# Splitting fifteen row buffers between two gather streams: one slot moved from the `v` ring to the `u` ring

## The reference

```python
sc = jnp.einsum('thcd,hcnd->thcn', qry, keys)      # 8 heads, 2 halves, 128 sub-keys
sv, si = lax.top_k(sc, PEER_TOPK)                  # 16 of each half
...
fv, fi = lax.top_k(cand.reshape(...), PEER_TOPK)   # 16 of 256 pairs
gate = jax.nn.softmax(fv, axis=-1)
ue = u[eidx]                                       # 8 x 16 = 128 rows of 1024 for each token
ve = v[eidx]
act = jax.nn.gelu(jnp.einsum('thkd,td->thk', ue, xb))
return jnp.einsum('thk,thkd->td', (gate * act), ve)
```

## Time and profile before

| | |
|---|---|
| median of 3 runs | 3388.74 us (3377.97 to 3389.66) |
| the profiled execution | 3388.74 us, its span 3386.9 us |
| PE (matmuls) busy | 2953.4 us, 87% |
| DVE busy | 2104.8 us, 62% |
| POOL busy | 2073.1 us, 61% |
| ACT busy | 1528.1 us, 45% |
| moved by DMA | 1222.63 MB, mean 361 GB/s |
| mean granted TensorE clock | 0.959 |

### The profile page before, as it was taken

The page is one execution under the profiler, slowest core; times in us unless marked ns, Lnnn a source line. Parts: engine busy times, 40 slices in busy tenths (PEclk is TensorE's granted clock), DMA queues, the critical chain, the costliest instruction groups (busy, mean ns, idle before and its releaser), DMA issues.

```text
span 3386.9 us, 31486 instructions
## 1 busy us (share of the span) xinstructions
PE 2953.4 (87%) x8213; PEld 1396.8 (41%) x8213; DVE 2104.8 (62%) x4852; ACT 1528.1 (45%) x4155; POOL 2073.1 (61%) x2162
## 2 busy tenths in 40 slices
PE   8888999889997899889997898789978997589976
PEld 6754444334443454335443443334433442244221
DVE  2345555856566566856685657766776668364594
ACT  2313653357423663357334753465336633252333
POOL 2003666666656666666667766776677667464675
PEclk9889999999999999999998999999989998798999
DMA  8307999999999999999999999999999999899998
GB/s 313 137 15 270 398 375 361 343 408 405 394 329 388 410 399 372 359 410 405 399 341 389 409 410 396 369 409 409 400 360 410 409 408 356 313 366 340 356 349 349
DMA packets 358876, 1222.63 MB, mean 361 GB/s; under 512 B 42747, under 2 KB 65244, under 8 KB 357404
## 3 DMA queue, kind: packets, MB, share of 16 engines
q0 software_dynamic: 308288, 1121.46, 85.5%
q1 hardware_dynamic: 22540, 66.55, 5.2%
q10 hardware_dynamic: 27872, 32.61, 2.9%
HBM read 1195.69 MB, written 25.79 MB: 361 GB/s over the span
## 4 chain that ended last, share of the span: by engine, by line
PE 47%; DMA 18%; DVE 15%; POOL 7%; issue 7%; ACT 5%; SPq 0%; ACTq 0%; DVEq 0%; POOLq 0%
PE ps L1091 24%; DMA rows<-in_peer_v,idx 11%; PE ps L973 7%; DMA rows<-in_peer_u,idx 5%; PE ps L857 5%; DVE rows L1497 5%; PE ps L956 4%; POOL rows L469 4%; POOL rows L479 3%; PE ps L810 2%; DVE r L1343 1%; DVE r L1338 1%; DVE r L1378 1%; PE ps L833 1%; DVE r L1379 1%
## 5 line engine op out<-in xcount | busy, mean ns | idle before, releaser
L1091 PE MATMUL ps<-rows,diag 128*128 128x512 f32 (+1 forms) x4224 | 2042.5, 620 | 329.8 <-DMA rows<-in_peer_v,idx 152.3
L1497 DVE CUSTOM_DVE_ANT_0 rows<-rows,ps 128x1024 f32<-128x1024 f32 x1056 | 1261.2, 1216 | 638.4 <-DMA rows<-in_peer_u,idx 635.6
L479 POOL DMA_INDIRECT rows<-in_peer_v,idx x1056 | 1028.5, 974 | 602.1 <-PE ps L1091 384.5
L469 POOL DMA_INDIRECT rows<-in_peer_u,idx x1056 | 1019.4, 965 | 603.4 <-issue 258.2
L1091 PEld LDWEIGHTS ps<-rows,diag 128*128 128x128 f32 (+1 forms) x4224 | 779.9, 194 | 1437.2 <-issue 1117.0
L747 ACT ACTIVATE act_g<-act_g 128x1 f32<-128x1 f32 x1056 | 211.0, 200 | 1069.6 <-DVE act_g L1497 1052.2
L753 ACT ACTIVATE diag<-ident,act_g 128x128 f32<-128x128 f32 x1024 | 411.2, 402 | 403.4 <-PE ps L1091 377.4
L749 ACT ACTIVATE act_g<-act_g,gate 128x1 f32<-128x1 f32 x1056 | 311.0, 294 | 34.3
L973 PE MATMUL ps<-w_sc,r 128*128 128x512 f32 (+1 forms) x576 | 282.8, 600 | 1.2 <-ACT r L663 1.2
L857 PE MATMUL ps<-rows 128*128 128x416 f32 (+1 forms) x704 | 242.2, 499 | 0.0
L857 PEld LDWEIGHTS ps<-rows 128*128 128x128 f32 x704 | 133.5, 191 | 106.1 <-issue 65.4
(11 more groups left out here) (269 smaller groups left out, 1836.3 us busy)
## 6 DMA issues: line engine op xcount, KB each, us to landing
rows<-in_w_in ACTq DMA_DIRECT2D x42, 512.0 KB, 6.5
rows<-in_peer_u,idx POOLq DMA_INDIRECT x1056, 8.7
rows<-in_peer_v,idx POOLq DMA_INDIRECT x1056, 8.6
r<-proj SPq DMA_DIRECT2D x7, 1344.0 KB, 10.9
proj<-staged ACTq DMA_DIRECT2D x44, 192.0 KB, 5.7
w_sc<-in_w_q_t SPq DMA_DIRECT2D x8, 1024.0 KB, 8.1
rows<-in_w_in POOLq DMA_DIRECT2D x14, 512.0 KB, 5.7
w_o<-in_w_in POOLq DMA_DIRECT2D x10, 512.0 KB, 7.4
```

The source lines that it names most:

```text
L469: nc.gpsimd.indirect_dma_start(ring[:, slot, :], None, a["peer_u"], bass.IndirectOffsetOnAxis(ap=idx[g % 2][:, k:k + 1], axis=0), engine_s ...
L479: nc.gpsimd.indirect_dma_start(ring[:, slot, :], None, a["peer_v"], bass.IndirectOffsetOnAxis(ap=idx[g % 2][:, k:k + 1], axis=0), engine_s ...
L1091: last = nc.tensor.matmul(Y[j][0:m, :], diag[:, n % DIAGS, 0:m], ring[:, slot, 512 * j:512 * (j + 1)], start=(k == 0), stop=(k == steps_of ...
L1497: V.tensor_tensor_reduce(ring[:, slot, :], ring[:, slot, :], hn_u, 1.0, 0.0, ALU.mult, ALU.add, col).then_inc(S["dots"], 1)
```

## The change

Slot 14 goes from the `v` ring to the `u` ring. The `u` ring then has 5 slots in tile 0, 6 in tiles 1 to 3 and 9 from tile 4; the `v` ring has 4, and 6 from tile 4. The tables `U_SLOTS` and `V_SLOTS` follow from that. Everything else is as before.

```diff
 RING = 15
-U_SETS = {0: (0, 1, 2, 3), 1: (8,), 4: (9, 10, 11)}
-V_SETS = {0: (4, 5, 6, 7, 14), 4: (12, 13)}
+U_SETS = {0: (0, 1, 2, 3, 14), 1: (8,), 4: (9, 10, 11)}
+V_SETS = {0: (4, 5, 6, 7), 4: (12, 13)}
 V_LAG = 2
```

## The result

The changed kernel takes 3413.86 us (median of 4 runs, 3412.94 to 3430.12), the kernel before 3386.98 us (median of 4, 3377.97 to 3389.66): a ratio of 1.0097, 95% interval 1.0075 to 1.0118, (by the two medians alone, 27 us or 0.8% more; the 36 executions of the changed kernel on record have a median of 3417.3 us). The forecast was 3410 us (3372 to 3450). The profiled execution took 3418.86 us, its span 3417.0.

What follows compares the result with a forecast made beforehand. The prediction took DMA gathers (2743 of 3387 us) as the bound, with PE, DVE and POOL's issue close behind. Its terms, -5 + 18 + 3 + 5 = +21 us on 3388.74, gave 3410 us, range 3372 to 3450.

Steps and rivals of the forecast that it cites:

- tile 0: First tile's period: the longer u ring lets POOL run a step further under DVE's pauses, a gain of 5 us.
- tiles 1 to 3: These three periods: one v slot less lengthens v waits and shortens the DMA queue, 6 us each, 18 us lost (6 to 54).
- tiles 4 to 6: Late tiles: the queue stays long enough for 409 GB/s; only top-k exits cost 1 us each, 3 us lost.
- tile 7 and the tail: Beside the sample tile's front: one step's transfer falls out of each of two POOL pauses, 5 us lost (0 to 10).
- the 3.36 us one: A v wait in 656 to 850, taken as typical of the seven over 1 us apart from the two longest.
- The rest of each period I cost at nothing: Tiles 1 to 3 outside the DMA-limited half: PE, then DVE, are the limit, so the lost slot costs nothing.
- the 2 us: Tiles 1 to 3, DMA-limited half: shorter landing time lowers 404 to 400 GB/s, 2 us a period, the lower bound.
- 5 against 5 ... there they are even: Tile 0 after the change: V+1 equals U, so neither ring binds first; V binds in every other tile.
- The lost slot held only a landed row: Rival, v ring: rows mostly landed already and waiting for PE, so only lower bounds are paid, 3392 us; chance 0.27.
- The u ring is the short one: Rival, where DVE stops: POOL meets the u wait first, so each tile period gains 2.6 us, 3363 us; chance 0.14.
- Every late v gather costs in full: Rival, all tiles: POOL gains only 0.12 us a step on DMA, so lateness stays, 3461 us; chance 0.15.
- The 3.2 us for one gather: Estimated time of one gather alone; by it three in flight fill the engines and four V slots are ample, near 3392 us.

Runs made afterwards that it cites:

- e1: Kernel before with only tile 0 given the changed split (u/v 5/4, then 5/5 and 8/7 as before); ratio to the kernel before 0.9996.
- e3: Kernel before with slot 14 taken from the v ring and left unused (u/v 4/4, 5/4, 8/6); ratio to the kernel before 1.0042.
- e10: Kernel before, own split, with V_LAG 1 in tiles 0 to 3 only and 2 from tile 4; 3377.86 us, ratio to the kernel before 0.9986.
- c2: The changed kernel, unchanged, run again beside the kernel before on a slower chip; ratio 1.0065.
- c1: The kernel before, unchanged, a single execution for its profile on a slower chip; 3552.85 us.
- e2: Kernel before with only tiles 4 to 8 given the changed split (u/v 4/5, 5/5, 9/6); ratio to the kernel before 1.0003.
- e4: Kernel before with slot 8 moved from the u to the v ring in tiles 1 to 3 only (u/v 4/6 there); ratio to the kernel before 1.0127.
- e8: Kernel before with slot 11 moved from the u to the v ring in tiles 4 to 8 only (u/v 7/8 there); ratio to the kernel before 1.0091.
- e7: Kernel before with its own split and V_LAG 1 in place of 2; ratio to the kernel before 0.9996.
- e5: The changed kernel with V_LAG 3 in place of 2; ratio to the kernel before 1.0045.
- e9: The changed kernel with V_LAG 1 in place of 2; ratio to the kernel before 1.0172.

## Why the prediction was right, and where it was not

**The total: right, in part by luck.** 21 us were said and 30.1 are between the two spans (27 between the medians). Taken one by one the terms missed by more: tile 0 by +8.8 us, tiles 1 to 3 by +6.8, tiles 4 to 6 by +3.4, tile 7 and the tail by -5.2, and the start, which had no term, came 4.8 us earlier. They partly cancel, which is luck. The mechanism, that the v ring becomes what stops POOL and the rate falls in tiles 1 to 3, held.

**Which ring would bind: right in kind.** V waits were to rise "by a hundred or more" and rose by 156; u waits were to fall well below 161 and fell to 46. The landing time came out at 7.1 us (said: near 7) in tile 1's first half and at 12.2 us (said: near 12) with 409 GB/s in the late tiles.

**Tiles 1 to 3, the term that carries the result: 18 us said, 24.8 us measured.** e1 and e3 show that the loss belongs to the v slot in these tiles: with the slot back it is gone, and without the gain of the u slot it is no larger by the ratio. The first part of the periods came nearly as said: 194 us at 391, 395 and 394 GB/s in place of 404, 403 and 405 is 6.2, 3.9 and 5.3 us, 15 where 18 were said, though inside it was another sum. The waits of the earlier trace rows grew by 0.3 to 1.7 us each and not by 2.5, new ones came beside them, and two of the five that I called like the 3.36 us one were 1.66 and 1.11 us. The step that failed is "The rest of each period I cost at nothing", with its reason that a landed row which waits for a full engine needs no slot behind it. The rest fell from 360, 371 and 367 GB/s to 354, 366 and 357, which by the same working is 3.4, 2.5 and 5.1 us, 11 together. The row that I used for it, 1150 to 1250, is not even in that part: it lies 107 to 207 us into tile 2's period, and it fell from 400 to 389 GB/s itself.

```profile
rows<-in_peer_v,idx POOLq DMA_INDIRECT x35, 6.9
```

That is the changed kernel's landing time there: 6.9 us at 389 GB/s, where before had 6.8 at 400 and e10 has 7.0 at 408. So the median time to landing does not fix the rate, and reading the 2 us from it was not sound.

**Tile 0: wrong sign.** A gain of 5 us was said, the profile has a loss of 3.8. The step that failed is "5 against 5 ... there they are even". It priced the sum's lag behind the dot by instruction times alone, 3 us. PE's program lets the sum run two steps behind DVE, and with it V binds as soon as it is not above U: the u waits went from 51.5 to 5.7 us and v waits took their place. By the later count tile 0 may even hold nine rows in place of eight, and c2's tile 0 took 374.8 us against c1's 374.7, no gain either. The count explains neither that nor the 3.8 us on the first chip; that stays open.

**Tiles 4 to 6: 3 us said, 6.4 measured** in the profiles, inside the bounds of 0 to 7.5, and not visible on the slower chips (e2). **Tile 7 and the tail: 5 us said, 0.2 less measured.** The long waits of the earlier trace rows went from 25.51 to 24.7 us and from 9.55 to 10.1: a stop that begins one row sooner did not leave a clearly longer hole. That nothing was lost for PE there is only argued from the period's time; I made no run for it.

**The rivals.** "The lost slot held only a landed row" is excluded by e1 and e3 for tiles 1 to 3; for the late tiles e2 agrees with it. "The u ring is the short one" is wrong for this change, and e4 and e8 show how near it was: a slot the other way costs 1.3% in tiles 1 to 3 and 0.9% from tile 4 on, most of it in the tail. "Every late v gather costs in full" falls with e7, where v waits are some 79 us longer (c1 to e7) and the ratio stays at 1.

**What is shown and what is not.** Shown is that the loss belongs to the v slot of tiles 1 to 3. That the time there follows the number of rows that both rings can hold at once is a rule found after eight of the kernels had run. It fits the ten profiles on the slower chips with e5 as the one exception, and it foretold e9; by it, the 6/4 split leaves one u slot idle there. It does not explain tile 0, e8's tail or where e10 gains. In 656 to 850 the rate is 404, 392 and 387 GB/s for 10, 9 and 8 rows (before, changed, e9), but 409 for e10, which also holds ten: the price of a missing row is seen as DMA's rate, and the count alone does not give the rate. The 3.2 us for one gather that the prediction worked out as an estimate from the Trainium skill, page "DMA: Bandwidth & Descriptors", section "Anatomy of one DMA — SWDGE (gpsimd) path", does not tell how many must be in flight: at some 7 us, over twice that, this case has 389 GB/s (changed) and 408 (e10) in 1150 to 1250, and no run here shows a gather alone.

## What to carry to other kernels

Where one engine issues two streams in a fixed order, a slot is useful only if both rings allow the same step; before pricing any wait, count the rows that may be in flight at the point where the consumers hold each other. Here the count ordered most of the kernels, with exceptions, so it chooses what to try and does not replace the run. Waits of one ring on the issuing engine say which ring binds and nothing of the price: between c1 and e7 some 70 to 80 us went from u waits to v waits at no cost. Their sum follows the time, as its busy time is fixed, and so it tells the loss only when the loss is known. Try the order of the streams (their lag) before the split, since it changes the count too and needs no memory.

## What the runs showed of the hardware

- Chips differ by 5% on this program. The kernel before takes 3383 to 3387 us on two occasions and 3539 to 3561 us on three; in c1 the DMA engines are 98% busy at 371 GB/s in 1900 to 2100, where the first chip shows 409 in a full stretch. The granted TensorE clock is lower as well, 0.940 over c1 against 0.959.
- A landing time of 14.5 us and one of 12.2 us give the same 409 GB/s. Near 7 us the median time to landing does not tell the rate: 392 GB/s at 7.1 us and 387 at 6.6 in 656 to 850, but 400 at 6.8 (before), 389 at 6.9 (changed) and 408 at 7.0 (e10) in 1150 to 1250.
- The start of the gathers varied between 286.9 and 294.3 us among kernels whose setup is the same.
